# Attention passes in another order by length, earlier reciprocals, a later wait for the last stores, and a rearranged final normalisation

## The reference, cut to what matters

```python
h = layer_norm(concat(meta, x))
mixed = concat(retention(4 heads), forgetting_attention(8 heads))   # then @ w_out
h = layer_norm(ALPHA * h + mixed @ w_out)
moe = swiglu(h, shared) + routed_experts(h)      # 64 experts, 6 per token
out = layer_norm(ALPHA * h + moe)[:, 16:]

def forgetting_attention(q, k, v, logf):         # causal, head width 64
    s = q @ k.T * 64 ** -0.5 + c_q - c_k         # c: running sum of logf
    p = softmax(where(k_pos <= q_pos, s, -1e30))
    return p @ v
```

## Time and profile before

| | us |
|---|---|
| median of 3 runs | 3201.52 (3197.09 to 3203.18) |
| the profiled execution: its own time | 3197.57 |
| its span, first to last instruction | 3195.7 |
| PE busy in the span | 3101.4 (97%) |
| DVE busy | 1109.9 (35%) |
| ACT busy | 686.0 (21%) |
| POOL busy | 641.3 (20%) |
| mean granted TensorE clock | 0.993 |

### The profile page before, as it was taken

How to read it: one execution, slowest core, us unless ns; L and a number is a source line. 1 busy time by engine, 2 the same in 40 slices (tenths; PEclk the granted TensorE clock), 3 DMA queues, 4 the chain that set the end, 5 groups by cost and what they waited for, 6 DMA issues and landing times.

```text
span 3195.7 us, 38048 instructions
## 1 busy us (share of the span) xinstructions
PE 3101.4 (97%) x14302; PEld 1994.9 (62%) x14302; DVE 1109.9 (35%) x3394; ACT 686.0 (21%) x1535; POOL 641.3 (20%) x631
## 2 busy tenths in 40 slices
PE   8999999999999899898999999999999999999997
PEld 4455555544445455554555767778877777877775
DVE  6423333330035656653677421111111111111117
ACT  2221111110024444442111111111111111111113
POOL 3200000000000010101354212222222223232324
PEclk9999999999999999999999999999999999999999
DMA  6421010011000103005434378788888888888885
GB/s 228 146 68 28 14 28 14 1 33 40 20 1 8 49 9 107 11 6 178 153 131 162 120 250 231 234 238 236 236 242 242 243 245 264 263 266 271 271 232 224
DMA packets 179111, 458.81 MB, mean 144 GB/s; under 512 B 24944, under 2 KB 97472, under 8 KB 153192
## 3 DMA queue, kind: packets, MB, share of 16 engines
q1 hardware_dynamic: 133872, 339.23, 30.0%
q0 software_dynamic: 42752, 108.72, 15.3%
q10 hardware_dynamic: 2304, 8.39, 0.7%
HBM read 342.33 MB, written 113.92 MB: 143 GB/s over the span
## 4 chain that ended last, share of the span: by engine, by line
PE 53%; DVE 0%; issue 0%; ACT 0%; POOL 0%; ACTq 0%; DVEq 0%; POOLq 0%
PE ps L2317 22%; PE ps L2261 11%; PE ps L2127 7%; PE ps L2245 4%; PE ps L2175 3%; PE ps L2258 2%; PE ps L2187 1%; PE ps L2147 1%; PE ps L2205 1%; PE ps L2137 0%; PE ps L2114 0%; DVE moe_fin L1613 0%; PE ps L2160 0%; PE ps L2159 0%; DVE moe_yt L1361 0%
## 5 line engine op out<-in xcount | busy, mean ns | idle before, releaser
L697 PE MATMUL ps<-ret_w,hT 128*128 128x512 f32 (+1 forms) x1088 | 465.0, 581 | 0.0
L2317 PEld LDWEIGHTS ps<-moe_xT,moe_wg 128*128 128x128 f32 x2048 | 352.8, 197 | 44.7 <-issue 40.7
L2317 PE MATMUL ps<-moe_xT,moe_wg 128*128 128x192 f32 (+22 forms) x2048 | 378.5, 338 | 0.0
L2317 PE MATMUL ps<-moe_xT,moe_wu 128*128 128x192 f32 (+22 forms) x2048 | 375.3, 337 | 0.0
L2261 PE MATMUL ps<-moe_wd,moe_hh 128*128 128x512 f32 (+12 forms) x800 | 366.5, 601 | 1.0 <-DVE moe_hh L1432 0.8
L2317 PEld LDWEIGHTS ps<-moe_xT,moe_wu 128*128 128x128 f32 x2048 | 353.4, 197 | 4.2
L697 PEld LDWEIGHTS ps<-ret_w,hT 128*128 128x128 f32 (+1 forms) x1088 | 196.0, 185 | 222.6 <-issue 215.5
L1879 POOL DMA_INDIRECT base_rows<-moe_yo,index x100 | 164.7, 1647 | 847.5 <-DVE moe_yo L1537 712.1
L1432 DVE TENSOR_TENSOR moe_hh<-moe_sl,ps 128x256 f32<-128x256 f32 (+19 forms) x144 | 53.7, 373 | 772.9 <-ACT moe_sl L1991 772.8
L2261 PEld LDWEIGHTS ps<-moe_wd,moe_hh 128*128 128x128 f32 (+12 forms) x800 | 136.9, 181 | 159.0 <-issue 149.5
L1053 PE MATMUL ps<-hT,fox_w 128*128 128x512 f32 (+1 forms) x576 | 226.9, 556 | 0.0
(11 more groups left out here) (251 smaller groups left out, 3589.9 us busy)
## 6 DMA issues: line engine op xcount, KB each, us to landing
moe_wg<-in_we_gate SPq DMA_DIRECT2D x64, 1024.0 KB, 4.9
moe_wu<-in_we_up SPq DMA_DIRECT2D x64, 1024.0 KB, 7.0
moe_wd<-in_we_down SPq DMA_DIRECT2D x64, 1024.0 KB, 7.8
fox_c<-ck SPq DMA_DIRECT2D x8, 1032.0 KB, 8.6
emb_xin<-in_x SPq DMA_DIRECT2D x16, 512.0 KB, 3.7
h_rows<-emb_hr SPq DMA_DIRECT2D x16, 512.0 KB, 2.9
ret_w<-in_w_in SPq DMA_DIRECT2D x16, 512.0 KB, 6.5
moe_yt<-h_rows SPq DMA_DIRECT2D x16, 512.0 KB, 5.2
```

The costliest lines, as they stand in the source:

```text
L697: ins = pe.matmul(ps[0:n, g % 2, lo:hi], hT[:, c, t0:t0 + n], wr[u][:, c, lo:hi], start=(c == 0), stop=(c == DC - 1))
L2317: ins = pe.matmul(out, w[:, c, f:FF:FC], xT[u][:, c, 0:n], start=(c == 0), stop=(c == DC - 1))
```

## The change

1. `order` is 7 5 3 1 0 2 4 6 in the first three pairs and 7 6 5 4 3 1 0 2 in the last. Units, steps, `lead` and the share of ACT and DVE in `back` follow from it by the same rules.
2. `inverse(n)` stands on DVE at i = 1 of the loop instead of i = 3 (for tile 7 it stays at 3).
3. The fox stage no longer waits for its stores. SP waits for the even ones ahead of `feathers(0)` and for the odd ones ahead of the third load of the moe stage; POOL waits for both ahead of a memset.
4. In the final stage: `centre` is one `tensor_scalar` on one column for each block instead of one `scalar_tensor_tensor` for a group. The statistics of blocks 10 to 13 move from DVE to ACT. Blocks 14 and 15 are centred and scaled by DVE alone (`direct_centre`, `direct_scale`), without ACT's `normalise`, `weight_rows` and the separate add. The calls stand in another order on DVE, ACT and POOL, and the stores go out as 0 to 12, 14, 13, 15.

```diff
-        order = [(p, t) for p in range(PAIRS) for t in range(TILES - 1, -1, -1)]
+        order = [(p, t) for p in range(PAIRS) for t in ((7, 5, 3, 1, 0, 2, 4, 6) if p + 1 < PAIRS else (7, 6, 5, 4, 3, 1, 0, 2))]
...
-            for b in range(2):
-                sp.wait_ge(o_s[b], 16 * (NT // 2))
...
-                    if i == min(3, max(len(groups[n]), lead[n]) - 1):
+                    if i == (3 if HALF[n] else min(1, len(groups[n]) - 1)):
                         inverse(n)
...
-        act_sums = (3, 7, 9)
+        act_sums = (3, 7, 9, 10, 11, 12, 13)
...
-                dve.scalar_tensor_tensor(out=shift2[:, lo:hi], in0=mv2[:, lo:hi, 0], scalar=-1.0, in1=rstd2[:, lo:hi],
-                                         op0=ALU.mult, op1=ALU.mult).then_inc(shifted2, 1)
+                for i in range(lo, hi):
+                    ins = dve.tensor_scalar(shift2[:, i:i + 1], mv2[:, i, 0:1], rstd2[:, i:i + 1], -1.0, ALU.mult, ALU.mult)
+                ins.then_inc(shifted2, 1)
...
-                if i in dve_adds:
-                    dve.wait_ge(scaled2, i + 1)
-                    dve.tensor_tensor(fin[i][:, :], fin[i][:, :], wide(ps[:, 0:2, :]), ALU.add).then_inc(shifted_by, 1)
+
+            def direct_centre(i):
+                dve.wait_ge(aggr2, d_upto[i + 1])
+                dve.scalar_tensor_tensor(out=fin[i][:, :], in0=fin[i][:, :], scalar=mv2[:, i, 0:1], in1=wide(ps[:, 6:8, :]),
+                                         op0=ALU.subtract, op1=ALU.mult).then_inc(centred2, 1)
+
+            def direct_scale(i):
+                dve.wait_ge(centred2, dve_adds.index(i) + 1)
+                dve.wait_ge(rstds2, next(g for g in range(len(GRP)) if i in GRP[g]) + 1)
+                dve.scalar_tensor_tensor(out=fin[i][:, :], in0=fin[i][:, :], scalar=rstd2[:, i:i + 1], in1=wide(ps[:, 0:2, :]),
+                                         op0=ALU.mult, op1=ALU.add).then_inc(shifted_by, 1)
...
+            sp.wait_ge(ahead.fox_out[0], ahead.fox_stored[0])
             feathers(0)
             hidden(0)
+            sp.wait_ge(ahead.fox_out[1], ahead.fox_stored[1])
...
             moments(2)
-            for i in range(4, 10):
+            for i in range(4, 8):
                 normalise(i)
+            moments(3)
+            for i in range(8, 10):
+                normalise(i)
+            moments(4)
             tail_silu(2, 0)
             for i in range(10, 12):
                 normalise(i)
             tail_silu(2, 1)
-            for i in range(12, 16):
+            moments(5)
+            moments(6)
+            for i in range(12, 14):
                 normalise(i)
```

More of the change, by code:

```diff
@@ L749, in fox_phase @@
         TILES = SEQ // QT
-        order = [(p, t) for p in range(PAIRS) for t in range(TILES - 1, -1, -1)]
+        order = [(p, t) for p in range(PAIRS) for t in ((7, 5, 3, 1, 0, 2, 4, 6) if p + 1 < PAIRS else (7, 6, 5, 4, 3, 1, 0, 2))]
+        assert all(sorted(t for x, t in order if x == p) == list(range(TILES)) for p in range(PAIRS))
         NT = len(order)
@@ L808, in fox_phase @@
         tab, ones_set = ahead.fox_tab, zero("ones_set")
-        w_s, v_s, c_s, o_s = ahead.fox_w, ahead.fox_v, ahead.fox_c, ph.zero_sems("o", 2)
+        w_s, v_s, c_s = ahead.fox_w, ahead.fox_v, ahead.fox_c
+        o_s = ahead.fox_out = [nc.alloc_semaphore(name=f"fox_out{b}") for b in range(2)]
+        ahead.fox_stored = [16 * (NT // 2)] * 2
         ahead.wo_s = [nc.alloc_semaphore(name=f"moe_wo_in{a}") for a in range(2)]
@@ L1644, in _ @@
             weight_rows(2)
+            tail_product(1, 1)
+            tail_sum(10)
             weight_rows(3)
-            tail_product(1, 1)
+            tail_sum(11)
             centre(2)
-            weight_rows(4)
-            tail_sum(10)
-            tail_sum(11)
-            for i in range(5, 8):
+            for i in range(4, 8):
                 weight_rows(i)
-            centre(3)
             weight_rows(8)
@@ L1656, in _ @@
             weight_rows(9)
+            centre(3)
             weight_rows(10)
@@ L1663, in _ @@
             centre(4)
+            direct_centre(14)
             tail_sum(15)
             weight_rows(12)
[L1666 removed]
             weight_rows(13)
[L1668 to L1670 removed]
+            direct_scale(14)
+            direct_centre(15)
+            direct_scale(15)
         @block.sync
@@ L1817, in _ @@
             pool.memset(route.ones[:, :], 1.0).then_inc(route.ones_set, 1)
+            for b in range(2):
+                pool.wait_ge(ahead.fox_out[b], ahead.fox_stored[b])
             pool.memset(blank[:, :], float(SEQ)).then_inc(blank_s, 1)
@@ L1946, in _ @@
                 shift_rows(i)
+            for i in range(5, 8):
+                shift_rows(i)
             inverse_std(3)
-            for i in range(5, 12):
+            for i in range(8, 12):
                 shift_rows(i)
```

27 lines of the change are left out of this document (12 added, 15 removed).

## The result

| | before | after |
|---|---|---|
| median of 5 runs, us | 3200.28 (3197.09 to 3203.18) | 3219.58 (3216.07 to 3220.47) |
| span of the profiled execution, us | 3195.7 | 3218.7 |
| mean granted TensorE clock | 0.993 | 0.986 |

A forecast was written before the change was run, and what follows sets the result against it. PE, busy for 97% of 3195.7 us, was taken to bound the kernel. The terms +15.3 + 3.0 + 7.8 - 1.5 - 8.0 gave +16.6 us, a forecast of 3216 us, range 3201 to 3229.

The forecast's parts named there:

- bare chain: Fox stage, longer tile next: PE waits through bias, maximum and exponentials after its last scores, 6.6 us for tile 4.
- Passes of the first three pairs: Fox stage: 6.1 us a pair gained, 11.2 lost to waits for exponentials; +5.1 a pair, +15.3 over three pairs.
- 0-2: Fox-stage pass of tile 0 with tile 2's scores: PE waits for tile 2's exponentials, 10.6 instead of 6.3 us, +4.3.
- S and T: Parts of a fox-stage pass: S, the next tile's scores, 7.7 to 0.9 us; T, its own tile's part, 20.3 to 3.5.
- The clock: Fox stage: half-clock falls behind each stop ahead of tiles 2 and 4 and half of those ahead of tile 6, +7.8 us.
- The early reciprocals: Fox stage: PE's waits at L1126, 3.5 us a pair, go; 1.7 of tile 0 and 0.8 of the rest counted as gain.
- Last pair: Fox stage, last pair from tile 3 on: 39.6 us instead of 36.7, +3.0 with rounding.
- The final stage: DVE's last instruction in the final stage ends at 3183.4, not 3191.4: -8.0 us, bounds -2 and -9.
- faster: Rival, fox stage: the longer tile's exponentials are done before PE needs them, no clock falls; -35, 3166 us; chance 0.06.
- only the clock is mis-sized: Rival, fox stage: the stops cost no more clock falls than before; +8.8, 3208 us; chance 0.14.
- the final stage gives 2: Rival: the final stage gives 2 instead of 8 us, as ACT's statistics or the columns hold it up; 3222; chance 0.10.
- order neutral: Rival: the new order leaves the fox stage even, ascending tiles' waits paying for tile 0's old wait; -9.5, 3192 us; chance 0.08.

The follow-up runs named there:

- the kernel with idle work: The changed kernel plus unread 128x512 products on PE behind the scatter, five where tile 4 follows tile 2, three where tile 6 follows tile 4: 3204.64 us.
- the kernel with half starts: The changed kernel, but tiles 4 and 6, where they follow a shorter tile, start with four groups of their first half: 3194.25 us.

## Why the prediction was right, and where not

The forecast was 3216, the median is 3219.6, and the likeliest case is the one that came. The mechanism is the one forecast: a bare chain, PE standing in front of the next transposes, and a clock that falls with the stops. That the sum came so near is in part luck: two of its terms were off and covered for each other, 26.1 us forecast for the fox stage and 26.9 measured.

- **Passes of the first three pairs, +15.3: too large.** The bare chain is as long as I took it (6.8 against 6.6 us). At the full clock the passes are, forecast first and where needed from the kernel with idle work: 7-5 25.5 and 24.9; 5-3 18.5 and 17.7; 3-1 12.7 and 12.8; 1-0 8.1 and 8.4; 0-2 10.6 and 10.5; 4-6 22.1 and 22.4; 6-7 24.5 and 23.6. 2-4 was forecast at 17.2; in this order with early reciprocals it was never seen at the full clock. 18.2 with a clock of 0.88 bounds it above, and 16.5 is an estimate of the lower bound (if the 3.4 us of half clock at its start cost half their length; the rest of the half clock lies in PE's stop). The sum is 137 to 138.5 instead of 139.2: +8 to +13 for three pairs. The steps that failed are S and T for the long tiles, 0.6 to 0.9 too long each in 7-5, 5-3 and 6-7.
- **0-2: right length, wrong wait.** I had PE wait for tile 2's exponentials. It waits 2.9 us at L1126 for the reciprocals behind tile 2's biases, until 1156.3 in this pair; tile 2's last exponential ends at 1156.9, when the spreading matmuls are just done. So the forecast chain was as long as I took it, but it is hidden behind another wait of the same length, and the sign that I named for this pass, a wait for L1006 of over 2 us, isn't there. The other sign that failed is L1126 "nearly without waits": 3.5 us a pair stayed.
- **The clock, +7.8: too small.** The three pairs took 433.2 us against 407.8 before, +25.5; with +8 to +13 for the passes, the clock is +12 to +17. I expected a fall behind half of the stops ahead of tile 6 and 1.6 us for each. In fact the clock was at half for 10.2 us around and behind all three stops of 4.4 us ahead of tile 4, and for 3.4 us at all three ahead of tile 6. The idle work is what shows it to be the stop: same waits, no fall. One reading of the earlier trace rows was wrong besides: the half clock in tile 0's pass starts with the pass, at 1056.7, behind tile 1's stops of 1.0 and 0.9 us, and not behind the 1.7 us at L1126, which come at the pass's end (1074.6). And the 1.9 us in tile 7 stand in all four pairs, with a fall behind them in two: the length of a stop alone doesn't say whether one follows.
- **The early reciprocals, a gain of about 0.8 us at L1126 and 1.7 in tile 0: wrong.** In the old order they gave 0.9, 0.2, 0.2 and 0.6 in tiles 6, 4, 1 and 0, took 0.8 and 0.5 in tiles 3 and 2 (1.2 each where the clock fell too): at the full clock 0.6 us a pair are left of 2.5, and with the clock next to nothing in the profiled execution, some 3 us in all by the median. In the new order the profiled runs have 4.5 us against them, most of it in tile 3's passes and in more half clock. I had looked at what waits for them, and not at what waits behind them on DVE.
- **Last pair, +3.0: +4.0 measured for the same passes.** From tile 3 on they took 36.9 us before and 40.9 after, where the clock was at half for 3.4 us; in the kernel with half starts they are 12.8, 8.4 and 10.5, and with tile 2 alone at 7.8 the sum is 39.4 at the full clock, +2.5. The whole pair is only 1.4 longer: tiles 6 and 4 gain 1.0 by the early reciprocals, and tile 7's pass had lost 1.6 to the half clock before and not after.
- **The boundary, -1.5: right** (-1.6).
- **The final stage, -8.0: right at DVE's end, -8.1, and 2.4 too much at the end.** I had read the last 4.3 us of the earlier trace rows as the store and what follows. The store had landed 1.6 us before the end; the span ended with GpSimd's drain, 6.8 us behind its last add. What counted was that add, and it came only 5.8 us sooner. Within the term the split was wrong: I gave the columns 1.6 us (2.14 less 0.5), having seen one of three long instructions, and DVE's new order the rest. The columns carry 2.5 to 4.3 of the 8.1 us (3.9 by the medians), and the new order, the direct forms and the statistics the rest, of which the statistics 1.2. DVE's order does remove PE's old stop, as I had it: it is gone with the group's instruction too. But without the columns another of 3.0 us comes behind the third `tail_up`. That the stage agrees to 0.1 us is luck in part as well: the same code took 71.6 to 75.3 us in the kernels above, by the clock and by PE's stops at its start.
- **The rule that I weighed.** The Trainium skill, SBUF — State Buffer, section "Who interferes with whom", holds that one VectorE instruction with two SBUF inputs and a reading GpSimd instruction exclude each other: 2.29, 1.11 and 2.30 us above agree, each ending with an add of GpSimd's. That `tensor_scalar` could wait as well, which the page ties to its two-port modes, did not happen in this form: fourteen columns of 0.2 us, eight of them beside GpSimd's adds.

Of the rivals, "faster" falls by the measured chain; "only the clock is mis-sized" had the sign wrong, the clock cost more; "the final stage gives 2" is nearer than I thought, since with the end of the program it gave 5.7 in the trace and 4.8 in the runs; "order neutral" holds only for the kernel with half starts, once the waits are out.

## What to carry to other kernels

When passes overlap, a longer successor behind a shorter one bares its whole chain. The matrix engine can pay for such a stop twice: here with 6.9 us a pair in waiting and 4.9 in the clock. Before an instruction is moved forward, read what then stands behind it on its own engine, not only who waits for it. And before work at the end is shortened, see which engine's last instruction the end of the program hangs on.
